# Compressed keys over projection blocks 2 to 5, linear attention over blocks 8 to 15, its steps ahead of the weight split

## The reference

```python
h = rmsnorm(x, norm1_g[l])
proj = h @ w_in[l]
(nq, kcm, vcm, ksl, vsl, kwn, vwn, ngate, gq, gk, gv, glr, gr, gate_a, gate_b) = jnp.split(proj, offsets, axis=-1)
# compressed keys and values: 15 blocks of 32 tokens, stride 16
blocks = t[:, :, blk_idx] + pos
hid = jax.nn.gelu(blocks.reshape(B, G, n_cmp, CMP_BLOCK * dh) @ w1)
kc_or_vc = hid @ w2
# gated linear attention, 4 heads, key width 128, value width 256
log_a = jax.nn.log_sigmoid(glr @ gla_w_decay[l] + gla_b_decay[l]) / GLA_TAU
attn = jnp.einsum('bhtd,bhsd,bhtsd->bhts', qi, ki, decay)
o = jnp.einsum('bhts,bhse->bhte', attn, vi) + ...
o = rmsnorm(o, norm_g)
y_gla = o * jax.nn.silu(r)
```

## Time and profile before

| what | us |
|---|---|
| median of 3 runs (lowest to highest) | 2573.32 (2573.13 to 2574.76) |
| the profiled execution, first to last instruction | 2571.0 |
| TensorE matmuls busy in it | 2469.6 (96%) |
| VectorE busy | 1503.7 (58%) |
| ScalarE busy | 1140.6 (44%) |
| GpSimd busy | 145.4 (6%) |

### The profile page before, as it was taken

One profiled execution on the slowest core, in us unless ns is written; L12 is line 12 of the kernel. 1 busy time (PEld: TensorE's weight loads), 2 busy tenths in 40 slices (PEclk: granted clock), 3 DMA queues, 4 the chain that ended last, 5 costly groups with the idle time before them and its releaser, 6 DMA issues.

```text
span 2571.0 us, 38713 instructions
## 1 busy us (share of the span) xinstructions
PE 2469.6 (96%) x14430; PEld 2185.9 (85%) x14430; DVE 1503.7 (58%) x2035; ACT 1140.6 (44%) x1013; POOL 145.4 (6%) x151
## 2 busy tenths in 40 slices
PE   7899978999999898999999999999999999999997
PEld 6788866788877778999999999999988888888885
DVE  5434466655545444588888866664545555555554
ACT  5434455444444333455455554544434443434342
POOL 0001054200000000000000000000000000000000
PEclk9899999999999999999999999999999999999999
DMA  7655644444445644465566565556676667676762
GB/s 268 229 176 218 220 154 141 174 149 156 150 180 209 228 152 175 161 201 200 193 215 207 201 240 213 206 222 243 223 258 243 248 237 250 231 258 228 254 236 99
DMA packets 84661, 530.12 MB, mean 206 GB/s; under 512 B 9856, under 2 KB 10112, under 8 KB 30448
## 3 DMA queue, kind: packets, MB, share of 16 engines
q1 hardware_dynamic: 58464, 423.65, 46.1%
q0 software_dynamic: 14896, 59.12, 6.7%
q10 hardware_dynamic: 11232, 46.37, 4.4%
HBM read 480.87 MB, written 48.23 MB: 206 GB/s over the span
## 4 chain that ended last, share of the span: by engine, by line
PE 85%; DVE 8%; issue 4%; ACT 3%; DMA 0%; ACTq 0%; DVEq 0%; POOL 0%; POOLq 0%
PE psum L1079 9%; PE psum L1081 9%; PE psum L1080 9%; PE psum L725 9%; PE psum L727 9%; PE psum L726 9%; PE psum L1028 7%; PE psum L1027 7%; PE psum L1029 7%; DVE w_lo L1126 2%; PE psum L1055 2%; ACT w_hi L402 1%; PE psum L862 1%; PE psum L782 1%; PE psum L983 1%
## 5 line engine op out<-in xcount | busy, mean ns | idle before, releaser
L1126 DVE TENSOR_TENSOR w_lo<-w_raw,w_hi 128x2048 fp32r<-128x2048 f32 x400 | 920.9, 2307 | 678.0 <-ACT w_hi L402 668.8
L402 ACT ACTIVATE w_hi<-w_raw 128x2048 fp32r<-128x2048 f32 x400 | 763.8, 1913 | 686.4 <-DMA w_raw<-in_w_units 472.6
L1027 PE MATMUL psum<-ynT_hi,w_hi 128*128 128x256 f32 x2048 | 581.2, 284 | 0.0
L1029 PE MATMUL psum<-ynT_lo,w_hi 128*128 128x256 f32 x2048 | 579.5, 283 | 0.0
L1028 PE MATMUL psum<-ynT_hi,w_lo 128*128 128x256 f32 x2048 | 579.5, 283 | 0.0
L1079 PE MATMUL psum<-w_hi,w_up 128*128 128x512 f32 x1024 | 399.2, 390 | 4.4 <-issue 4.4
L1080 PE MATMUL psum<-w_lo,w_up 128*128 128x512 f32 x1024 | 398.9, 390 | 0.0
L1081 PE MATMUL psum<-w_hi,w_low 128*128 128x512 f32 x1024 | 398.8, 389 | 0.0
L1028 PEld LDWEIGHTS psum<-ynT_hi,w_lo 128*128 128x128 f32 x2048 | 393.1, 192 | 0.0
L1027 PEld LDWEIGHTS psum<-ynT_hi,w_hi 128*128 128x128 f32 x2048 | 393.1, 192 | 0.0
L1029 PEld LDWEIGHTS psum<-ynT_lo,w_hi 128*128 128x128 f32 x2048 | 393.0, 192 | 0.0
(11 more groups left out here) (303 smaller groups left out, 2365.4 us busy)
## 6 DMA issues: line engine op xcount, KB each, us to landing
w_raw<-in_w_units SPq DMA_DIRECT2D x400, 1024.0 KB, 4.8
hid_scratch<-hst ACTq DMA_DIRECT2D x32, 512.0 KB, 5.8
h_in<-hid_scratch POOLq DMA_DIRECT2D x16, 1024.0 KB, 5.5
g_tab<-tab_scratch POOLq DMA_DIRECT2D x16, 1024.0 KB, 11.3
proj_scratch<-evac ACTq DMA_DIRECT2D x24, 512.0 KB, 4.3
tab_scratch<-gate_a ACTq DMA_DIRECT2D x10, 1024.0 KB, 4.1
tab_scratch<-gate_b ACTq DMA_DIRECT2D x6, 1024.0 KB, 3.9
x_nat<-in_x POOLq DMA_DIRECT2D x2, 2048.0 KB, 8.5
```

The costliest lines, as they stand in the source:

```text
L402: act.activation(w_hi[:, s % SPLIT, :], w_raw[:, s % RAW, :], ACT.Copy).then_inc(hi_done, 1)
L1027: pe.matmul(out, uh, h2T_hi[:, c, :], start=c == 0, stop=False, skip_group_check=True)
L1029: ins = pe.matmul(out, uh, h2T_lo[:, c, :], start=False, stop=c == KC - 1, skip_group_check=True)
L1126: dve.tensor_tensor(w_lo[:, s % SPLIT, :], w_raw[:, s % RAW, :], w_hi[:, s % SPLIT, :].bitcast(F32), ALU.subtract).then_inc(lo_done, 1)
```

## The change

The heads of the linear attention move from blocks 12 to 15 (four units each) to blocks 8 to 15 (eight units each), and the plain stretch of blocks 4 to 11 shrinks to blocks 6 and 7. The preparation is spread over the 16 units of blocks 2 to 5. In both, ScalarE's and VectorE's extra steps now stand ahead of the split of their step's unit. TensorE's half-units go. The loops become written-out code, and GpSimd's gate on stored blocks is split: q and k are loaded once blocks 0 to 3 are stored, v and r once blocks 0 to 7 are. No instruction of arithmetic is added or taken away. Sparse attention and everything behind it keep their places.

```diff
-A_BLOCKS = 12
+A_BLOCKS = 8
...
             for k in range(2):
-                pool.wait_ge(stored[k], 16 * B_KSL // 2)
+                pool.wait_ge(stored[k], 16 * (B_GK // 2 + 1))
...
+                for k in range(2):
+                    pool.wait_ge(stored[k], 16 * B_KSL // 2)
...
-            for k in range(2 * UPB):
-                hi(2 * UPB + k + AHEAD, k + AHEAD)
-                if k == 0:
+            for k in range(4 * UPB):
+                if k == 1:
                     act.wait_ge(pe_prep, 1)
...
-                if k in (3, 4):
+                if k in (7, 8):
...
-                if k in (5, 6):
+                if k in (11, 13):
...
-                if k == 7:
+                if k == 15:
...
+                hi(2 * UPB + k + AHEAD, k + AHEAD)
...
             def gla_slot(h, k):
-                if k == 0:
+                if k == 1:
                     act.wait_ge(g_qkt, h + 1 + FIRST)
...
+                if k == 3:
                     act.wait_ge(g_vr_in, h * 32 + 32)
...
-                if k == 2:
+                if k == 5:
                     act.wait_ge(g_o, h + 1 + FIRST)
...
-                if k == 3:
+                if k == 6:
                     decays(h + 1)
+                if k == 7:
                     act.wait_ge(g_yt, h + 1)
...
+            for h in range(GLA_H):
+                for k in range(2 * UPB):
+                    gla_slot(h, k)
+                    hi(base + h * 8 + k + AHEAD, k + AHEAD)
+                    if k % UPB == UPB - 1:
+                        evacuate(A_BLOCKS + h * 2 + k // UPB, k // UPB)
...
+            parts = {0: 0, 2: 1, 6: 3, 7: 4, 10: 5, 12: 6, 14: 7}
+            for k in range(4 * UPB):
+                proj_unit(2 * UPB + k, k % UPB, k // UPB % 2, 2 + k // UPB)
+                if k in parts:
+                    prep_part(parts[k])
...
-                if (k, half) == (0, 1):
+                if k == 0:
...
-                if (k, half) in ((1, 1), (2, 0)):
-                    t = k - 1
+                if k in (2, 3):
+                    t = k - 2
...
-                if (k, half) == (2, 1):
+                if k == 4:
...
-                if (k, half) == (3, 1):
+                if k == 6:
...
+            for h in range(GLA_H):
+                for k in range(2 * UPB):
+                    proj_unit(base + h * 8 + k, k % UPB, k // UPB, A_BLOCKS + h * 2 + k // UPB)
+                    gla_part(h, k)
...
```

More of the change, by code:

```diff
@@ L312, in _ @@
             pool.wait_ge(g_one, 1)
[L313 to L333, removed]
@@ L514, in _ @@
             base = A_BLOCKS * UPB
[L515 to L525, removed]
+            for h in range(GLA_H):
+                for k in range(2 * UPB):
+                    gla_slot(h, k)
+                    hi(base + h * 8 + k + AHEAD, k + AHEAD)
+                    if k % UPB == UPB - 1:
+                        evacuate(A_BLOCKS + h * 2 + k // UPB, k // UPB)
+            base = (A_BLOCKS + 8) * UPB
             with act.Fori(0, NSA_G) as g:
@@ L707, in _, with unit @@
                 pe.sem_inc(s, FIRST)
-            def unit(n, k4, par, xh, xl, kc0, first, last, free, half=None):
+            def unit(n, k4, par, xh, xl, kc0, first, last, free):
                 s = k4 % SPLIT
[L713 to L719, removed]
+                pe.wait_ge(hi_done, n + 1)
+                pe.wait_ge(lo_done, n + 1)
+                if first and free is not None:
+                    pe.wait_ge(*free)
+                for c in range(CU):
                     rh, rl = w_hi[:, s, c * NB:(c + 1) * NB], w_lo[:, s, c * NB:(c + 1) * NB]
@@ L791, in prep_part, with gla_part @@
                     ins.then_inc(pe_prep, 1)
-            for k in range(2 * UPB):
[L794 to L802, removed]
-                if (k, half) == (0, 1):
+            parts = {0: 0, 2: 1, 6: 3, 7: 4, 10: 5, 12: 6, 14: 7}
[3 more added lines that the diff above has]
+                    prep_part(parts[k])
+            for k in range(2 * UPB):
+                proj_unit(6 * UPB + k, k % UPB, k // UPB, 6 + k // UPB)
+            def gla_part(h, k):
+                if k == 0:
                     pe.wait_ge(g_in, h * 32 + 32)
@@ L1191, in _ @@
                 lo(UPB + k + AHEAD, k + AHEAD)
-            for k in range(2 * UPB):
-                lo(2 * UPB + k + AHEAD, k + AHEAD)
-                if k == 1:
+            for k in range(4 * UPB):
+                if k == 3:
                     dve.memset(bT[:, GLA_H, :], 0.0)
@@ L1220, in _ @@
                     ins.then_inc(dve_prep, 1)
-            with dve.Fori(2, A_BLOCKS // 2) as i:
-                for k in range(2 * UPB):
-                    lo(i * 8 + (k + AHEAD), k + AHEAD)
+                lo(2 * UPB + k + AHEAD, k + AHEAD)
+            for k in range(2 * UPB):
+                lo(6 * UPB + k + AHEAD, k + AHEAD)
             def gla_slot(h, k):
-                if k == 0:
+                if k == 1:
                     dve.wait_ge(g_exp, h + 1)
@@ L1242, in gla_slot @@
                         dve.tensor_copy(att_T[:, 2, :], psum[:, 4, 0:P]).then_inc(g_a01, 1)
+                if k == 5:
+                    gla_output(h)
+                if k == 7:
+                    gla_lower(h)
             def gla_output(h):
@@ L1261, in _ @@
             base = A_BLOCKS * UPB
[L1262 to L1272, removed]
-                    gla_lower(i * 2 + hp)
-                step.leave(GLA_H // 2)
+            for h in range(GLA_H):
+                for k in range(2 * UPB):
+                    gla_slot(h, k)
+                    lo(base + h * 8 + k + AHEAD, k + AHEAD)
             def scores_max(h, j):
```

63 lines of the change are left out of this document (38 added, 25 removed).

## The result

The changed kernel takes 2518.85 us in the median of 4 runs (2518.55 to 2522.96), the kernel before 2574.04 beside it (2573.13 to 2577.43): a ratio of 0.9785, 95% interval 0.9771 to 0.9799. That is 55.2 us, 2.1%. Forecast were 2515.7 us and 57.6 us of gain, in a range of 2508 to 2534.

A forecast was written before the change was run, and what follows sets the result against it. TensorE, busy 96% of the span, bounds the kernel, so only its holes can go: 37.1 + 16.9 + 3.6 = 57.6 us off the 2571.0 us span gives 2513.4, and 2.3 more the median, 2515.7 us; range 2508 to 2534.

The forecast's parts named there:

- Heads: Four linear-attention heads: 38.7 us lost to waits and slow clock, 1.6 of it staying, so 37.1 us gained.
- the walk: One head followed link by link with traced durations: ends at 49.8 us, smallest slack 2.3 us, TensorE does not wait.
- Head 0: First linear-attention head: 1.6 us of waiting stays there.
- the two links named: In the first head: the wait for loading q and k, 0.9 us with start-up, and `qL` 0.7 us late.
- Preparation: Blocks 2 to 5: 17.7 us lost before, 0.8 left at the rotation, so 16.9 us gained.
- rival A: Clock dips stay in preparation, heads and sparse attention's start: 20.9 us back, 2536.6 us; chance 0.10.
- Start of sparse attention: First three units of sparse attention: 2.0 us idle and about 1.6 of slow clock go, 3.6 us gained.
- The split behind the steps: Weight split (`hi`, `lo`, load) in the heads: runs three units ahead, least margin 8.7 us, so it holds nothing up.
- Rival C: Raw buffers become the bound in the heads: up to 66.5 us a head, 2582.5 us, slower; chance 0.05.
- Rival B: `qL` or `att_T` stays 2 us late in every head, with slow clock: 15.6 us back, 2531.3 us; chance 0.10.
- Writing out the loops: Loops turned into written-out code: gives 0 in the sum, as units inside a loop already take 5.44 us.
- Rival D: Clock dips later in sparse attention vanish as well: up to 7 us more gain, 2509 us; chance 0.05.

The follow-up runs named there:

- the third profile: The changed kernel run unaltered a third time, beside the kernel without the three left waits; measured 2518.12 us.

## Why the prediction was right

- **Heads.** Forecast 238.0 - 37.1 = 200.9 us, measured 200.2. TensorE at the places of the walk: 49.65 a head against 49.8. `qL` had 3.3 us of slack against 3.5, the sums of the two tiles 2.0 each against 2.3.
- **Head 0.** Forecast 1.6 us left, measured 51.28 - 49.65 = 1.63 in the first profile, at the two links named; in the third profile it was 2.6, with the first sum late as well.
- **Preparation.** Forecast 16.9 gained with 0.8 us left at the rotation; measured 16.5, and 1.2 left there (1.0 of wait). Both short groups took 7.1 us: the clock had followed the waits, and rival A, that it would keep dipping, falls for these stretches, since the granted clock is 1.00 through both with all their short groups. The Trainium skill (TensorE: Matmul & The Clock Gate, A second HAM failure mode) tells of micro-idles between groups of matmuls that make the clock swing, in a bf16 kernel. This trace neither confirms nor refutes that: heads 1 to 3 show no idle at the edges of the groups (busy 49.65 of 49.65 us). In the merge, where waits remain, the clock still falls.
- **Start of sparse attention.** Forecast 3.6, measured 3.9.
- **The split behind the steps.** Forecast 8.7 us of margin; the lead of two units shows that at least one unit's time (5.4) was there, in heads 1 to 3. Rival C falls with it. Rival B, a `qL` or `att_T` wait in every head, falls with the list of waits, which has none in heads 1 to 3; the doubled `qL` shows how near it was.
- **Writing out the loops** brought nothing where it can be read alone: the plain units take 5.44 us in both kernels.
- **The term that was mis-sized** is the loss of the kernel before, "17.7 us" in the preparation and "3.6" at the start of sparse attention. Both were read from one execution and are mostly clock; a second execution lost 15.0 and 1.8, and 0.5 more in the heads. In the mean of the two the kernel before is 2.1 us shorter up to unit 67 than the execution I read, which is nearly all of the 2.4 us between 57.6 and 55.2. That two executions settle the mean is not shown. Rival D, a gain further on from another phase of the clock, has no sign that holds: the stretches behind unit 67 scatter either way. Rival A in full (2536.6) lies outside the stated range, which was said to hold most of it.
- **What I took wrongly beside it:** 5.28 us as the cost of `qL`. It is the cost beside GpSimd. The sum did not suffer, since GpSimd's work stayed beside it.

## What to carry to other kernels

When a busy engine waits in many places for short chains on others, walk one period with measured durations and give each link the distance it needs; work that is long in units (8 in place of 4) costs the busy engine nothing. Judge an order only together with its distance: ScalarE's steps ahead of the split cost 18.6 us at four units a head and belonged to the gain at eight. Follow every moved step round the loop it sits in (split, load, split) before calling a neighbour independent, and read losses that are mostly clock from more than one profile.

## What the runs showed of the hardware

Elementwise instructions that read two operands from SBUF slow each other across VectorE and GpSimd: the 128x2304 product took 5.32 us on VectorE beside GpSimd's product and 2.56 alone, and two `lo` beside GpSimd's work took 6.00 in place of 4.6. The Trainium skill (SBUF — State Buffer, Who interferes with whom) says that a VectorE instruction with two SBUF inputs contends with a GpSimd instruction that reads SBUF, and calls it an exclusive lock. The first case agrees: GpSimd's product ran until 284.49, 2.9 us behind the start of VectorE's at 281.59, and 2.9 and 2.56 make 5.5, near the 5.32. GpSimd pays in the same way. Its differences in the changed kernel, shortest, median and longest in ns:

```profile
L307 POOL TENSOR_TENSOR dec<-bT x40: 603/620/2692, 172.7 to 392.9; 128x256 f32<-128x256 f32 x40
```

The one that starts at 173.27 us, behind the start of a `lo` at 172.81, takes 2.69 us in place of 0.62: it ends half a microsecond behind that `lo`, which itself takes 2.67 in place of 2.29.

In the heads with the steps behind the split, a wait of some 1.8 us once a head left the granted clock at 1.00 (heads 1 to 3); head 0, with waits of 2.4 and 2.0, had 0.97.

The granted clock of the same instructions in the same order differed between executions: 150.72 us at 0.97 and 156.33 at 0.94 in the merge. So one profile of this kernel can tell differences down to some 5 us, 0.2%.
